# Delta rule on two 64x64 diagonal blocks in 128 rows, and weight remainders formed over the raw weights

## The reference, cut to what matters

```
diff = gc[..., :, None] - gc[..., None, :]            # 64 x 64 per chunk and head
decay = exp(where(tril, diff, -inf))
m = where(strict, (k_beta @ k^T) * decay, 0)          # Gram
sol = solve(m + I, [v_beta, k_beta * exp(gc)])        # u, w
a_qk = (q @ k^T) * decay
# then over the chunks, one after another:
v_new = u_i - w_i @ S
o_i = (q_i * exp(g_i)) @ S + a_i @ v_new
S = S * exp(g_last) + k_dec^T @ v_new
```

## Time and profile before

| | us |
|---|---|
| median of 3 runs | 1082.01 (1078.73 to 1083.92) |
| the profiled execution | 1080.94 |
| its span | 1079.3 |
| PE busy (matmul) | 1016.9 (94%) |
| PE weight loads | 799.7 (74%) |
| DVE busy | 637.0 (59%) |
| ACT busy | 296.3 (27%) |

### The profile page before, as it was taken

How to read it: one execution, slowest core, us unless ns; L and a number is a source line. 1 busy time by engine, 2 the same in 40 slices (tenths; PEclk the granted TensorE clock), 3 DMA queues, 4 the chain that set the end, 5 groups by cost and what they waited for, 6 DMA issues and landing times.

```text
span 1079.3 us, 13803 instructions
## 1 busy us (share of the span) xinstructions
PE 1016.9 (94%) x4854; PEld 799.7 (74%) x4854; DVE 637.0 (59%) x1128; ACT 296.3 (27%) x534; POOL 72.3 (7%) x140
## 2 busy tenths in 40 slices
PE   5999999879999999999999998989999969999998
PEld 4876655558777777777788887777888857787887
DVE  5235765535567666666543434768778788634543
ACT  4132343413222222222111103643222325502220
POOL 1000000000000000000000000000000000000000
PEclk9999999989999999999999999989999979999999
DMA  9853322044445555555556553435432200113343
GB/s 316 258 183 130 113 94 87 1 156 156 160 172 175 195 175 175 190 179 175 196 176 213 176 182 131 156 138 174 145 129 98 98 1 1 39 47 125 123 143 111
DMA packets 35440, 153.52 MB, mean 142 GB/s; under 512 B 3904, under 2 KB 4672, under 8 KB 26944
## 3 DMA queue, kind: packets, MB, share of 16 engines
q0 software_dynamic: 19584, 71.31, 20.4%
q1 hardware_dynamic: 12384, 75.50, 19.6%
q10 hardware_dynamic: 3424, 6.04, 1.7%
HBM read 148.64 MB, written 4.19 MB: 142 GB/s over the span
## 4 chain that ended last, share of the span: by engine, by line
PE 58%; DVE 22%; ACT 8%; issue 7%; DMA 3%; DVEq 1%; ACTq 0%; POOLq 0%
PE bank L498 42%; DVE LO L1459 4%; DMA HI<-wstream 3%; ACT YC L1086 3%; DVE YC L1466 3%; DVE AB L1462 2%; DVE YC L1470 2%; PE bank L785 2%; DVE YC L1475 1%; DVE LO L1324 1%; PE bank L612 1%; ACT AH L1092 1%; PE bank L793 1%; PE bank L551 1%; PE bank L631 1%
## 5 line engine op out<-in xcount | busy, mean ns | idle before, releaser
L498 PE MATMUL bank<-GH,HI 128*128 128x512 f32 x720 | 295.3, 410 | 17.2 <-DVE AB L1462 8.7
L498 PE MATMUL bank<-GH,LO 128*128 128x512 f32 x720 | 282.4, 392 | 0.0
L498 PE MATMUL bank<-GL,HI 128*128 128x512 f32 x720 | 282.2, 392 | 0.0
L1324 DVE TENSOR_TENSOR LO<-RAW,HI 128x1024 fp32r<-128x1024 f32 x92 | 112.2, 1221 | 150.7 <-DMA HI<-wstream 141.8
L498 PEld LDWEIGHTS bank<-GH,HI 128*128 128x128 f32 x720 | 136.2, 189 | 60.4 <-DVE AB L1462 17.3
L498 PEld LDWEIGHTS bank<-GH,LO 128*128 128x128 f32 x720 | 135.7, 188 | 29.9
L498 PEld LDWEIGHTS bank<-GL,HI 128*128 128x128 f32 x720 | 136.3, 189 | 24.0
L486 POOL DMA_DIRECT2D HI<-wstream x132 | 69.9, 529 | 981.9 <-PE bank L498 972.0
L1086 ACT ACTIVATE YC<-AB,PAR 128x512 f32<-128x512 f32 x44 | 35.9, 816 | 145.5 <-DVE AB L1462 145.5
L498 PE MATMUL bank<-AH,HI 128*128 128x512 f32 x176 | 70.3, 400 | 0.4 <-DVE AB L1462 0.4
L498 PE MATMUL bank<-AH,LO 128*128 128x512 f32 x176 | 69.3, 394 | 0.0
(11 more groups left out here) (274 smaller groups left out, 1435.7 us busy)
## 6 DMA issues: line engine op xcount, KB each, us to landing
HI<-wstream POOLq DMA_DIRECT2D x136, 512.0 KB, 3.9
RAW<-wstream SPq DMA_DIRECT2D x66, 1024.0 KB, 4.8
X<-x_t SPq DMA_DIRECT2D x8, 256.0 KB, 13.3
RAW<-wstream SPq DMA_DIRECT2D x4, 512.0 KB, 13.0
out_t<-X ACTq DMA_DIRECT2D x8, 256.0 KB, 2.3
XR<-out_t ACTq DMA_DIRECT2D x8, 256.0 KB, 2.7
out_t<-XR SPq DMA_DIRECT2D x8, 256.0 KB, 2.4
CON<-consts ACTq DMA_DIRECT2D x1, 704.0 KB, 6.1
```

Source lines behind the costliest of these rows:

```text
L498: mm = pe.matmul(out, a, b, start=(first and n == 0), stop=(last and n == 2))
L1324: dve.tensor_tensor(LO[:, u % RING, :], RAW[:, u % RING, :], HI[:, u % RING, :].bitcast(F32), ALU.subtract).then_inc(unit_split, 1)
```

## The change

1. Every chunk matrix is kept as a stack of two 64x64 blocks: chunk 0 in rows 0 to 63, chunk 1 in rows 64 to 127, 64 columns per head. AQK, NT, XI, XT, YM, the masks and the identity for them (IDC) are half as wide. VectorE's and ScalarE's instructions on them handle 256 columns where they handled 512, and YM's 64 where it handled 128.
2. TensorE does each product once per head and chunk, in the quadrant of the array that its rows and its output rows name: chunk 0 in rows and columns 0 to 63, chunk 1 in rows and columns 64 to 127. The two transposes (Y at level 0, X) become products with IDC.
3. The solve has the keys' product of chunk 0, then the values', then the keys' of chunk 1, with a wait on chunk 0's keys between. In the scan, the chunk matrix's part of the output is done for each chunk, over its 64 rows.
4. LO lies over RAW: VectorE writes the remainder where the raw weights stood. So RAW is loaded unit by unit (512 KB), and a slot's raw load waits, like HI's, for TensorE to be done with the unit in it.

```diff
-        RAW = place("RAW", [P, RING, 1024], F32)
+        RAW_AT = here[0]
+        RAW = place("RAW", [P, RING, 1024], F32)
+        LO = place("LO", [P, RING, 1024], F32R, RAW_AT)
         HI = place("HI", [P, RING, 1024], F32R)
-        LO = place("LO", [P, RING, 1024], F32R)
...
             with sp.Fori(1, UNITS // 4) as i:
-                for s in range(2):
-                    sp.wait_ge(unit_split, 4 * i + (2 * s - 2))
-                    sp.dma_start(RAW[:, 2 * s:2 * s + 2, :],
-                                 wstream[bass.ds(2 * i + s, 1)].rearrange("o p (a n) -> p (o a) n", a=2))\
-                      .then_inc(w_landed[s], 16)
+                for s in range(RING):
+                    sp.wait_ge(unit_done, 4 * i + (s - RING + 1))
+                    sp.dma_start(RAW[:, s, :],
+                                 wstream[bass.ds(2 * i + s // 2, 1), :, 1024 * (s % 2):1024 * (s % 2 + 1)]
+                                 .rearrange("o p n -> p (o n)")).then_inc(w_landed[s], 16)
...
+            def by_chunk(out, left, right):
+                for h in range(4):
+                    for c in range(2):
+                        r = rows_of(c)
+                        mm = pe.matmul(out[r, cut(h)], left[r, h, :], IDC[r, :] if right is None else right[r, h, :],
+                                       start=True, stop=True)
+                return mm
...
                 for h in range(4):
-                    mm = pe.matmul(A[:, blk(h)], KT[:, h, blk(b)], KT[:, h, blk(b)], start=True, stop=True)
+                    for c in range(2):
+                        mm = pe.matmul(A[rows_of(c), cut(h)], KT[:, h, chunk(b, c)], KT[:, h, chunk(b, c)],
+                                       start=True, stop=True)
...
-                for h in range(4):
-                    if l == 0:
-                        mm = pe.transpose(A[:, blk(h)], NT[:, s, h, :], IDENT)
-                    else:
-                        mm = pe.matmul(A[:, blk(h)], NT[:, s, h, :], XI[:, s, h, :], start=True, stop=True)
-                mm.then_inc(y_mm, 1)
+                by_chunk(A, NT[:, s, :, :], XI[:, s, :, :] if l else None).then_inc(y_mm, 1)
...
-                    mm = pe.matmul(banks_for(b)[1][:, blk(h)], XT[:, s, h, :], YM[:, s, h, :], start=True, stop=True)
+                by_chunk(banks_for(b)[1], XT[:, s, :, :], YM[:, s, :, :]).then_inc(z_mm, 1)
...
-                    mm = pe.transpose(banks_for(b)[1][:, blk(h)], XI[:, b % 2, h, :], IDENT)
+                by_chunk(banks_for(b)[1], XI[:, b % 2, :, :], None).then_inc(xt_mm, 1)
...
+                def keys(c):
+                    r = rows_of(c)
+                    for h in range(4):
+                        mm = pe.matmul(B[:, P * h + CH * c:P * h + CH * (c + 1)], KBE[r, s, h, :], XT[r, s, h, :],
+                                       start=True, stop=True)
+                    mm.then_inc(w_mm, 1)
+                keys(0)
                 for h in range(4):
-                    mm = pe.matmul(A[:, blk(h)], XT[:, s, h, :], VBT[:, s, h, :], start=True, stop=True)
+                    for c in range(2):
+                        r = rows_of(c)
+                        mm = pe.matmul(A[r, blk(h)], XT[r, s, h, :], VBT[r, s, h, :], start=True, stop=True)
                 mm.then_inc(u_mm, 1)
-                for h in range(4):
-                    mm = pe.matmul(B[:, blk(h)], KBE[:, s, h, :], XT[:, s, h, :], start=True, stop=True)
-                mm.then_inc(w_mm, 1)
+                pe.wait_ge(w_mm, 2 * b + 1)
+                keys(1)
...
                 for h in range(4):
                     o = PS[2][:, P * h + r:P * h + r + 64]
-                    mm = pe.matmul(o, ST[:, h, :], QT[:, h, CH * i:CH * (i + 1)], start=(r == 0 and h == 0), stop=False)
-                    if r:
-                        mm = pe.matmul(PS[2][:, blk(h)], VT[:, h, blk(b)], AQK[:, b, h, :], start=False, stop=(h == 3))
+                    pe.matmul(o, ST[:, h, :], QT[:, h, CH * i:CH * (i + 1)], start=(r == 0 and h == 0), stop=False)
+                    mm = pe.matmul(o, VT[r:r + 64, h, blk(b)], AQK[r:r + 64, b, h, :], start=False,
+                                   stop=(r == 64 and h == 3))
```

More of the change, by code:

```diff
@@ L310, in build @@
         EG = place("EG", [P, 4, T], F32, arena + 24 * KB)
-        AQK = place("AQK", [P, NB, 4, P], F32, arena + 32 * KB)
+        AQK = place("AQK", [P, NB, 4, CH], F32, arena + 32 * KB)
         KDEC = place("KDEC", [P, NB, 4, P], F32, arena + 40 * KB)
@@ L314, in build @@
         RSP = place("RSP", [P, 2, T], F32R, TR + 17 * KB)
[L315 to L318, removed]
+        NT = place("NT", [P, 2, 4, CH], F32, TR)
+        XI = place("XI", [P, 2, 4, CH], F32, TR + 4 * KB)
+        XT = place("XT", [P, 2, 4, CH], F32, TR + 8 * KB)
+        YM = place("YM", [P, 2, 4, CH], F32, TR + 12 * KB)
         KBE = place("KBE", [P, 2, 4, P], F32, TR + 16 * KB)
@@ L375, in heads, with chunked @@
             return ap.rearrange("p (h c) -> p h c", h=4)
+        def chunked(bank):
+            return heads(bank[:, 0:4 * CH])
         x_landed = [sem(f"x_landed{k}") for k in range(KC)]
@@ L380, in build @@
         sg_landed = sem("sg_landed")
-        first_landed = [sem(f"first_landed{u}") for u in range(RING)]
-        w_landed = [sem("w_landed0"), sem("w_landed1")]
+        w_landed = [sem(f"w_landed{s}") for s in range(RING)]
         hi_landed = [sem(f"hi_landed{s}") for s in range(RING)]
@@ L744, in blk, with cut, rows_of, chunk @@
                 return slice(P * b, P * (b + 1))
+            def cut(h):
+                return slice(CH * h, CH * (h + 1))
+            def rows_of(c):
+                return slice(CH * c, CH * (c + 1))
+            def chunk(b, c):
+                return slice(P * b + CH * c, P * b + CH * (c + 1))
+            def by_chunk(out, left, right):
[5 more added lines that the diff above has]
+                return mm
             def banks_for(b):
@@ L756, in block_products @@
                 for h in range(4):
-                    mm = pe.matmul(A[:, blk(h)], KT[:, h, blk(b)], KT[:, h, blk(b)], start=True, stop=True)
+                    for c in range(2):
+                        mm = pe.matmul(A[rows_of(c), cut(h)], KT[:, h, chunk(b, c)], KT[:, h, chunk(b, c)],
+                                       start=True, stop=True)
                 mm.then_inc(g_mm, 1)
                 for h in range(4):
-                    mm = pe.matmul(B[:, blk(h)], KT[:, h, blk(b)], QT[:, h, blk(b)], start=True, stop=True)
+                    for c in range(2):
+                        mm = pe.matmul(B[rows_of(c), cut(h)], KT[:, h, chunk(b, c)], QT[:, h, chunk(b, c)],
+                                       start=True, stop=True)
                 mm.then_inc(aq_mm, 1)
@@ L1205, in _ @@
                     act.wait_ge(xt_mm, step(b, l) + 1)
[L1206 removed]
+                    act.activation(XT[:, b % 2, :, :], chunked(PS[3 + 2 * (b % 2)]), ACT.Copy)\
                        .then_inc(xt_made, 1)
@@ L1546, in block_decays @@
                 dve.wait_ge(cols_made, 1)
-                then(dve.tensor_tensor(AQK[:, b, :, :], EG[:, :, P * b:P * (b + 1)], over_head(COLS[:, b, 0, :]),
-                                       ALU.subtract))
-                dve.tensor_tensor(AQK[:, b, :, :], AQK[:, b, :, :], GNEG.unsqueeze(1).to_broadcast([P, 4, P]),
+                for c in range(2):
+                    r = slice(CH * c, CH * (c + 1))
+                    part = dve.tensor_tensor(AQK[r, b, :, :], EG[r, :, P * b + CH * c:P * b + CH * (c + 1)],
+                                             COLS[r, b, 0, :].unsqueeze(2).to_broadcast([CH, 4, CH]), ALU.subtract)
+                then(part)
+                dve.tensor_tensor(AQK[:, b, :, :], AQK[:, b, :, :], GNEG.unsqueeze(1).to_broadcast([P, 4, CH]),
                                   ALU.add).then_inc(d_made, 1)
@@ L1553, in block_products @@
                 s = b % 2
-                A, B = (heads(PS[n + 2 * s][:, :]) for n in (2, 3))
+                A, B = (chunked(PS[n + 2 * s]) for n in (2, 3))
                 dve.wait_ge(d_exp, b + 1)
@@ L1748, in _constants @@
     con[:, K_CAUSAL + 384:K_CAUSAL + 512] = np.where(i[None, :] <= i[:, None], 0.0, NEG)
-    same = i[:, None] // CH == i[None, :] // CH
-    con[:, K_GNEG:K_GNEG + P] = np.where(same & (i[:, None] <= i[None, :]), 0.0, NEG)
+    row, col = i[:, None] % CH, i[None, :CH]
+    con[:, K_GNEG:K_GNEG + CH] = np.where(row <= col, 0.0, NEG)
+    con[:, K_IDC:K_IDC + CH] = row == col
     for l in range(LEVELS):
-        pair = i[:, None] >> (l + 1) == i[None, :] >> (l + 1)
-        con[:, K_LV + P * l:K_LV + P * (l + 1)] = pair & ((i[:, None] >> l & 1) == 1) & ((i[None, :] >> l & 1) == 0)
+        pair = row >> (l + 1) == col >> (l + 1)
+        con[:, K_LV + CH * l:K_LV + CH * (l + 1)] = pair & ((row >> l & 1) == 1) & ((col >> l & 1) == 0)
     return con
```

32 lines of the change are left out of this document (14 added, 18 removed).

## The result

The changed kernel takes 1103.93 us (median; 1101.47 to 1104.46) against 1080.37 (1076.37 to 1083.92) for the kernel before on the same chip: a ratio of 1.0209 [1.0186, 1.0232], 23.6 us slower. Forecast were 1098 and slower, in 1086 to 1118. The profiled execution took 1103.86, its span 1102.2.

What follows compares the result with a forecast made beforehand. TensorE bounds the first preparation and the scan; VectorE and ScalarE count only in the second preparation. +5.5 - 2.5 + 11.5 + 3 = +17.5 on 1080.94 gives 1098.4, forecast 1098 us, range 1086 to 1118.

Steps and rivals of the forecast that it cites:

- The pairs: Quadrant steps: 16 records run as 8 pairs, one per array half, at 0.06 us a pair, 0.48 in all.
- The change of shape: Narrow steps between full-width products: about 0.35 us for going in and out, making a quadrant step 0.83.
- The fourth rival: Quadrant steps: TensorE pays nothing for changing between its tiles; sum -9.6, 1071 us; chance 0.10.
- First preparation: Two blocks, bound by TensorE: Y and Z -1.2, X and Y at level 0 +5.5, T1 -1.3, W +3.1 less 0.6; sum +5.5.
- W: The solves in the first preparation: 1.79 now, 3.35 after, +1.55 each, with 0.6 off for idle TensorE.
- Second preparation: Beside the attention: VectorE -3.5, Y or Z -2.7, X +1, solves +2.7; sum -2.5, bounds -8 and +5.
- Scan: Eight small groups per chunk, seven shape changes inside; 3.7 to 4.2 us a chunk; +10 to +14, taken as +11.5.
- The weights: LO over RAW loads raw weights later, beside HI's loads; six landings in the chain; +3 (-1 to +9).
- six places: HI landings in the chain: +1 to +2 at 230.03, +1 at 274.82, +1 at 113.17, two others -0.5 each.
- the two "-0.5": Two HI landings that coincided with a 1 MB raw pair meet 0.5 MB afterwards: -0.5 each.
- +1 in all: In the preparation VectorE waits for HI at every unit, without TensorE waiting for VectorE: +1 in all.
- The third rival: Late raw loads hold VectorE 1 to 1.5 us per unit, a third reaching TensorE; +12, about 1107; chance 0.10.

Runs made afterwards that it cites:

- the weights alone: The kernel before with LO over RAW and raw loads unit by unit when the product is done, chunk matrices unchanged; 1090.41 us, ratio 1.0107.
- The delta rule alone: The changed kernel with the old ring of weights (LO beside RAW, raw pairs loaded when remainders are formed); 1091.44 us, ratio 1.0106.
- the changed kernel with the move: The whole change, with the remainders of units 27, 28 and 98 moved back in VectorE's order; 1087.56 us, ratio 1.0068.
- the fourth experiment: Changed kernel with old weight ring; in each quadrant step, chunk 0's four products come before chunk 1's instead of alternating; 1116.51 us, ratio 1.0339.
- the third: Changed kernel with old weight ring; "sb" in two groups instead of eight, state products first, then chunk-matrix products; 1084.89 us, ratio 1.0039.
- seventh: Changed kernel with old weight ring and grouped scan, plus two steps between two quarters instead of one in both preparations; 1080.17 us, ratio 0.9999.
- eighth: Changed kernel with old weight ring and grouped scan, plus steps of the two blocks paired in the first preparation only; 1078.77 us, ratio 1.0007.
- eleventh run: Changed kernel with old weight ring, grouped scan, steps paired in the first preparation, and three remainders moved back in VectorE's order; 1061.45 us, ratio 0.9833.
- the moved base: The kernel before, with the remainders of units 27, 28 and 98 moved behind additions in VectorE's order; 1063.88 us, ratio 0.9854.
- the tenth experiment: The kernel before with LO over RAW, late raw loads, and three remainders moved back in VectorE's order; 1075.37 us, ratio 0.9969.

## Why the prediction was right in direction and low by 6

**The pairs: right.** 0.06 a pair was expected; the records show 0.058. A page of the Trainium skill, TensorEngine Tiling (Array Packing), Restrictions and Gotchas, says that different row tiles cannot access one PSUM bank at the same time. The trace disagrees: two row halves wrote one bank in pairs 7 ns apart, each record lasting 0.22 us.

**The change of shape: right, in two places.** A step holds TensorE 0.61, and the quarter behind it grew by 0.20: together 0.81 for the 0.83 of the sum. Two steps side by side saved 0.40, for 0.35. The fourth rival (no cost) is out.

**First preparation: +3.6 for +5.5.** By the rows, 20 steps of Y and Z at -0.08 and 14 of X at +0.38 make +3.7, for the +4.3 expected. T1's four groups took 2.01 for 3.49, -1.5. W takes 3.09 for 1.79, +1.3 each where I had 1.55. Timeline of TensorE after, a solve up to the next block's T1:

```profile
869.45 1.10 PE L831 MATMUL bank<-XT,KBE 64*128 64x64 f32 x8
870.49 1.09 PE L839 MATMUL bank<-VBT,XT 64*64 64x128 f32 x16
871.51 1.10 PE L831 MATMUL bank<-XT,KBE 64*128 64x64 f32 x8
872.54 0.68 PE L781 MATMUL bank<-KT 128*64 128x64 f32 x15
```

These make +4.8, and 1.2 less stayed. The larger part is at the solves: the two together grew by 1.8 and not by 2.6, since TensorE stood idle for 0.65 beside one of them before and for nothing after; the prediction took off 0.6 for that. The other 0.4 is open.

**Second preparation: -3.9 for -2.5.** VectorE's instructions are as short as forecast. Lines of the kernel after from 750 us on, by shape (busy us, mean ns):

```profile
L1605 DVE SCALAR_TENSOR_TENSOR YM<-bank,SM,CON 128x64 f32<-128x64 f32 x96 | 20.3, 274 | 6.6 <-PE bank L765 6.3
L1616 DVE TENSOR_TENSOR XI<-XI,bank 128x256 f32<-128x256 f32 x20 | 8.2, 410 | 2.8 <-PE bank L765 2.7
```

342 The earlier trace rows less 68 was expected, 274 measured. How the saving splits between the engines was not separated. The -3.9 also owes something to the one execution before: its 84.10 is the longest of the six traces with wide matrices (four others have 83.1 to 83.2, one 81.8), and the six with narrow ones in the same order have 78.9 to 80.8.

**Scan: +11.9 for +11.5, but not all by my mechanism.** The eight "sb" sum to 30.4 us for 19.9: +10.5 from records and changes of shape, with 0.4 of the clock in the last of them. "sb" itself came out at 3.75, the low end of the 3.7 to 4.2 of the prediction, where +11.5 stood for the middle. The other 1.4 was not in the sum: it is the clock, and that the stage met the 11.5 so closely is luck. Stretches of the kernel after, behind the first "sb" (955.20 to 958.95) and at the end of the last (1034.18 to 1038.31):

```profile
957.00:959.00 2.00, 2.00 (x15) 1.74 (x15) 0.00 (x0) 0.00 (x0) 0.00 (x0) 0.99 0.00 0
959.00:961.00 2.00, 2.00 (x6) 1.61 (x6) 1.12 (x4) 0.00 (x0) 0.00 (x0) 0.50 0.00 0
961.00:963.00 2.00, 2.00 (x12) 1.81 (x11) 0.69 (x1) 0.00 (x0) 0.48 (x1) 0.66 0.00 0
```

```profile
1036.00:1038.00 2.00, 2.00 (x14) 1.86 (x14) 0.08 (x1) 0.88 (x2) 0.00 (x0) 0.86 0.00 0
1038.00:1040.00 2.00, 2.00 (x6) 1.49 (x6) 1.12 (x4) 0.86 (x2) 0.00 (x0) 0.50 0.00 0
```

In both places the clock falls to the lower level, 1.2 GHz, for some 3 us, though TensorE is busy in all 2.00 us of each row. The first costs the scan about 1.7 us. The second lies almost wholly behind the last "sb": it is 1.5 of the 2.8 us by which the part after the scan grew, and the weights alone have the other 1.3. What TensorE did just before was the row of small groups that change shape. The delta rule alone shows one such fall (0.50 at 1016 to 1018), the changed kernel with the move two (945 and 1014), the fourth experiment one of 10 us (969) and one of 3 (1041); all seven begin within an "sb" of small groups or less than 1 us behind it. The scans of the four kernels with the grouped "sb" (the third, seventh, eighth and eleventh run) and of the six with the old one all stand at 1.00. That the fine groups cause it is inferred from this division; most "sb" of small groups show no fall.

**The weights: the step that failed.** I gave them +3 (-1 to +9). Measured alone they cost 10.3, and 11.5 on the moved base. I had priced the landings in the chain with one median, "5.0 for the later of the two". As a median it is right: 5.0 on the page. But at a wait that matters, often two units end within 1 us, as at 277 and 665, and then four loads of 512 KB run at once: 6.60 for 4.88, and 7.33 where the kernel before has 2.50 at 661.94 (its part in the chain; the load took 3.52). That last one is also a place without a price: my sum speaks of six places and prices five. Of the two "-0.5", one shows in the chain (5.06 for 5.72); the other place, 725.39, left the chain without making its units shorter. The "+1 in all" for the preparations holds only with wide matrices: the first takes 98.3 to 98.8 in three kernels with late loads for 97.3 in three with early ones, but 100.94 for 100.86 with narrow matrices, and the second shows no difference (83.2 and 83.1).

And the cost was not in six places. The times between the ends of units, the weights alone against before, show +2.3 from unit 12 to 24, +0.3 from 24 to 28, +2.3 from 30 to 33, +1.2 and +2.3 from 97 to 101, and +1.3 behind the scan. The feed-forward loop and the down projection up to its last step show nothing, as I had expected; that last step is 1.6 shorter and unit 103 1.6 longer, where a stretch at the lower clock stands in the one execution and is absent or shorter in the other. Taking two of the places away (the tenth experiment) left the sum as it was. The third rival, +12 for the weights, was nearest in size, though not in its mechanism: it wanted each landing over 2 us later, and the median rose by 1.1. The total is low by 6 only, though this term is low by 7 to 8, because the delta rule's stages came out 3 below their sum.

## What to carry to other kernels

Halving a matrix that is half zeros saves TensorE nothing when each of its small products then needs more records and a change of tile shape (about 0.14 each, 0.35 to 0.40 in and out, beside 0.11 for a full record): count the changes first, and group equal shapes. A buffer shared to save space moves its load to a later moment; price that by the landings at the waits in the chain, where loads bunch, and not by the median. Look in the kernel before for what waits in its own order: moving three remainders was worth 15 us, more than the whole question of the shapes. And read the granted clock of each stage before giving a difference to the products in it: in the fourth experiment it can account for more than half of the 25 us.

## What the runs showed of the hardware

- Products in diagonal quadrants of the array, two halves of the rows into one bank, start in pairs 7 ns apart, 0.058 us a pair over 64 columns. With the halves one behind the other the same 16 records take 0.89 instead of 0.61, still under the 1.08 that is estimated without overlap.
- In the scan the granted clock fell to its lower level for 3 to 10 us while TensorE was busy throughout (2.00 of 2.00 us in the rows above), seven times in four kernels, each time within or just behind groups of two records of changing shape, and never in the ten scans without such groups.
- An HI load of 512 KB lands after 3.9 us in median in the kernel before, where half of them have nothing beside them, after 5.0 with one other of its size always beside it, and after 6.6 to 7.7 where four are under way (at 277 and 665).
